# A chunked recurrence in a two-block model: triangular blocks as 32x32 tiles, with their copies shared by two engines

## What is computed

```python
def step(state, inp):
    r_t, w_t, k_t, v_t, kk_t, b_t = inp
    sa = jnp.einsum('bhij,bhj->bhi', state, kk_t)
    state = (state * w_t[:, :, None, :] - sa[..., None] * b_t[:, :, None, :]
             + v_t[..., None] * k_t[:, :, None, :])
    y_t = jnp.einsum('bhij,bhj->bhi', state, r_t)
    return state, y_t
s0 = jnp.zeros((B, H, N, N), f32)
_, y = lax.scan(step, s0, (seq_first(rh), seq_first(wh), seq_first(kh),
                           seq_first(vh), seq_first(kk), seq_first(bh)))
```

## Time and profile before

| | |
|---|---|
| median of 3 runs | 1327.83 us |
| profiled execution, its own time | 1327.68 us |
| its span in the trace | 1325.9 us |
| busy share of PE, DVE, ACT, POOL | 91%, 56%, 46%, 37% |
| mean granted TensorE clock | 0.955 |
| the scan, from its first `w_of` to its last `keep_y` | 330.31 to 454.43 us |

### The profile page before, as it was taken

How to read it: one execution, slowest core, us unless ns; L and a number is a source line. 1 busy time by engine, 2 the same in 40 slices (tenths; PEclk the granted TensorE clock), 3 DMA queues, 4 the chain that set the end, 5 groups by cost and what they waited for, 6 DMA issues and landing times.

```text
span 1325.9 us, 18744 instructions
## 1 busy us (share of the span) xinstructions
PE 1206.0 (91%) x7186; PEld 941.2 (71%) x7186; DVE 745.0 (56%) x1183; ACT 611.1 (46%) x1005; POOL 484.7 (37%) x395
## 2 busy tenths in 40 slices
PE   4699887878999869989999999999999999998977
PEld 4466666656888647777777776777888888876656
DVE  4575996771344373456676657447258234656673
ACT  3576543532222333565655646446111244555664
POOL 1242333426355014433332333434344445532221
PEclk8899898989799879999999999999999999999989
DMA  6642245333010414422222222243233333322101
GB/s 227 216 120 61 58 96 149 111 103 116 10 19 15 145 34 129 134 80 79 64 65 65 64 66 79 80 148 99 72 96 98 99 103 97 95 69 62 48 32 64
DMA packets 198874, 118.13 MB, mean 89 GB/s; under 512 B 27965, under 2 KB 187270, under 8 KB 198534
## 3 DMA queue, kind: packets, MB, share of 16 engines
q1 hardware_dynamic: 194976, 110.58, 28.7%
q10 hardware_dynamic: 3814, 6.40, 1.3%
HBM read 102.28 MB, written 14.68 MB: 88 GB/s over the span
## 4 chain that ended last, share of the span: by engine, by line
PE 37%; issue 24%; POOL 12%; DVE 10%; ACT 2%; POOLq 0%; DMA 0%; ACTq 0%; DVEq 0%
POOL b_w_lo L498 12%; PE banks L587 9%; PE banks L588 9%; PE banks L589 9%; PE banks L856 4%; DVE b_suffix L2403 2%; DVE b_problems L1982 1%; PE banks L831 1%; DVE b_sum_squares L1980 1%; PE banks L1128 1%; PE banks L850 1%; DVE b_softplus L2397 1%; DVE b_sv L2026 1%; PE banks L880 1%; PE banks L940 1%
## 5 line engine op out<-in xcount | busy, mean ns | idle before, releaser
L498 POOL TENSOR_TENSOR b_w_lo<-b_w_raw,b_w_hi 128x512 fp32r<-128x512 f32 x320 | 426.0, 1352 | 762.8 <-ACT b_w_hi L1226 762.8
L587 PE MATMUL banks<-b_a_lo,b_w_hi 128*128 128x512 f32 x1280 | 527.9, 412 | 57.0 <-DVE b_a_lo L1862 20.8
L589 PE MATMUL banks<-b_a_hi,b_w_lo 128*128 128x512 f32 x1280 | 508.0, 397 | 0.0
L588 PE MATMUL banks<-b_a_hi,b_w_hi 128*128 128x512 f32 x1280 | 507.9, 397 | 0.0
L587 PEld LDWEIGHTS banks<-b_a_lo,b_w_hi 128*128 128x128 f32 x1280 | 245.5, 192 | 135.8 <-issue 38.6
L1226 ACT ACTIVATE b_w_hi<-b_w_raw 128x1024 fp32r<-128x1024 f32 x160 | 168.8, 1055 | 267.0 <-PE banks L589 265.9
L589 PEld LDWEIGHTS banks<-b_a_hi,b_w_lo 128*128 128x128 f32 x1280 | 245.6, 192 | 54.4
L588 PEld LDWEIGHTS banks<-b_a_hi,b_w_hi 128*128 128x128 f32 x1280 | 246.6, 193 | 45.5
L1602 ACT ACTIVATE b_exps<-banks,b_stats 128x128 f32<-128x128 f32 (+3 forms) x64 | 33.2, 524 | 58.4 <-DVE b_stats L2197 58.4
L1537 ACT ACTIVATE b_a_hi<-b_x_t,b_params 128x512 fp32r<-128x512 f32 x48 | 33.9, 719 | 53.6 <-DVE b_x_t L2082 53.1
L2082 DVE TENSOR_TENSOR b_x_t<-b_x_t,banks 128x512 f32<-128x512 f32 x32 | 22.0, 686 | 59.7 <-PE banks L589 59.7
(11 more groups left out here) (310 smaller groups left out, 1546.7 us busy)
## 6 DMA issues: line engine op xcount, KB each, us to landing
b_w_raw<-rw_w_in SPq DMA_DIRECT2D x32, 512.0 KB, 4.1
b_w_raw<-da_w_in SPq DMA_DIRECT2D x32, 512.0 KB, 4.0
b_w_raw<-w_in_a SPq DMA_DIRECT2D x32, 512.0 KB, 4.0
b_w_raw<-pe_w_gate SPq DMA_DIRECT2D x16, 512.0 KB, 4.2
d_ple<-b_ple_out ACTq DMA_DIRECT2D x16, 256.0 KB, 2.6
b_w_raw<-rw_w_out SPq DMA_DIRECT2D x8, 512.0 KB, 4.2
b_ple_in<-d_ple SPq DMA_DIRECT2D x2, 2048.0 KB, 10.5
b_w_raw<-da_w_out SPq DMA_DIRECT2D x8, 512.0 KB, 4.0
```

The source lines that it names most:

```text
L498: m = pool.tensor_tensor(WLO[:, u % 2, ks], WRAW[:, u, ks], WHI[:, u % 2, ks].bitcast(F32), ALU.subtract)
L587: pe.matmul(dst, hi, a_lo[:, k_act, :], start=first, stop=False)
L588: pe.matmul(dst, hi, a_hi[:, k_act, :], start=False, stop=False)
L589: return pe.matmul(dst, lo, a_hi[:, k_act, :], start=False, stop=last)
```

## The change

Every block product becomes 16 matmuls with a 32x32 stationary operand, each on its own place in the array, the even head's beside the odd head's. No zeros are loaded, and each of the three steps computes only the half that is used, so `z_of`, `b_of`, `u_of` become `first_u`, `rest_w`, `second_u`. The even heads' W and U now lie in other PSUM banks than the odd heads' (banks 3 and 4, crosswise). Between the steps ACT copies the even heads' 32 rows and DVE the odd heads' 32 rows. The buffer `TRI` holds all chunks' blocks, so it needs no clearing and no reuse: POOL's memsets go, and SP issues all 48 loads in a row; `first_u` of the first chunk waits for 12 of them, that of the third chunk for the other 36. One half of each chunk's output is copied by ACT in place of DVE. DVE's `keep_products` is split into four parts a chunk, which stand between its new copies.

```diff
-    (DBX,) = phase([("blocks", [P, 2, 2, NT, P])], tail_at)
+    (TRI,) = phase([("blocks", [P, NC, 2, NT, BL])], tail_at)
...
         for c in range(NC):
-            if c >= 2:
-                sp.wait_ge(sem("u_mm"), c - 1)
-            got = sem(f"blocks_in{c % 2}")
+            got = sem(f"blocks_in{min(c // 2, 1)}")
             for h in range(2):
...
-                    sp.dma_start(DBX[bp, c % 2, 0, :, bp], D_T[c, :, h, bt, bt].rearrange("j s t -> s j t")).then_inc(got, 16)
...
+                    sp.dma_start(TRI[block_rows(h, b), c, 0], D_T[c, :, h, bt, bt].rearrange("j s t -> s j t")).then_inc(got, 16)
...
-            if 3 <= n < 7:
-                pool.memset(DBX[:, (n - 3) // 2, (n - 3) % 2], 0.0).then_inc(sem("blocks_zero"), 1)
...
-        def block_product(dst, n, c, src, start):
+        def block_product(c, kind, dst, src, start):
+
             for j in range(NT):
-                m = pe.matmul(dst[:, tile_cols(j)], DBX[:, c % 2, n, j, :], src[:, j, :], start=start and j == 0, stop=True,
-                              skip_group_check=True)
+                for h in range(2):
+                    out, bo, rhs, bi = dst(h, j) + src(h, j)
+                    m = pe.matmul(out[block_rows(h, bo), tile_cols(j)], TRI[block_rows(h, bi), c, kind, j, :], rhs,
+                                  start=start and j == 0, stop=True, skip_group_check=True,
+                                  tile_position=(h * CH + bi * BL, h * CH + bo * BL))
             return m
...
+        def first_u(c):
+            if c in (0, 2):
+                pe.wait_ge(sem(f"blocks_in{c // 2}"), 16 * 6 * (2 if c == 0 else NC - 2))
+            pe.wait_ge(sem("w1_kept"), 2 * c + 2)
+            block_product(c, 0, lambda h, j: (UB[h], 0), lambda h, j: (WX[block_rows(h, 0), j, :], 0), True
+                          ).then_inc(sem("u1_mm"), 1)
...
-            z_of(c)
+            first_u(c)
+            if c + 1 < NC:
+                rows_of(c, 0)
+            rest_w(c)
             if c + 1 < NC:
                 products(c + 1, 1)
-            b_of(c)
-            if c + 1 < NC:
-                rows_of(c, 0)
-            u_of(c)
+            second_u(c)
...
             act.wait_ge(sem("w_mm"), c + 1)
-            keep(WX[:, :, :], BANK[3], "w_kept")
-            act.wait_ge(sem("z1_mm"), c + 1)
-            keep(ZX[:, :, :], BANK[4], "z_kept")
-            act.wait_ge(sem("b_mm"), c + 1)
-            keep(WX[:, :, :], BANK[3], "w_kept")
+            keep(WX[first], BANK[3][first], "w1_kept")
+            act.wait_ge(sem("u1_mm"), c + 1)
+            keep(UV[first, :, 0, :], BANK[4][first], "u1_kept")
...
+            act.wait_ge(sem("yx_mm"), c + 1)
+            keep(YT[low, :, c * CH:(c + 1) * CH], BANK[6 + c % 2][low].rearrange("p (j t) -> p j t", t=CH), "y_even")
...
+            dve.wait_ge(sem("w_mm"), c + 1)
+            keep(WX[first], tiles(BANK[4][first]), "w1_kept")
             if c + 1 < NC:
-                for g in range(2):
-                    keep_products(c + 1, g)
-            dve.wait_ge(sem("u_mm"), c + 1)
-            dve.tensor_copy(UV[up, :, 1, :], tiles(BANK[4][up])).then_inc(sem("u_odd"), 1)
+                keep_products(c + 1, 0, 0)
+            dve.wait_ge(sem("u1_mm"), c + 1)
+            keep(UV[first, :, 1, :], tiles(BANK[3][first]), "u1_kept")
             if c + 1 < NC:
+                keep_products(c + 1, 0, 1)
```

More of the change, by code:

```diff
@@ L172, in gn_tile_bank, with block_rows @@
     return (0, 1, 2, 3, 4, 5, 7, 0)[j]
+def block_rows(h, b):
+    return slice(h * CH + b * BL, h * CH + (b + 1) * BL)
 def row(buf, j):
@@ L873, in s_of, with second_u @@
+        def second_u(c):
+            pe.wait_ge(sem("w2_kept"), 2 * c + 2)
+            block_product(c, 0, lambda h, j: (UB[h], 1), lambda h, j: (WX[block_rows(h, 1), j, :], 1), True
+                          ).then_inc(sem("u2_mm"), 1)
         def s_of(c):
@@ L2006, in _, with keep_products @@
         strict = cst("strict_s").unsqueeze(1).to_broadcast([P, 4, CH])
-        def keep_products(c, g):
+        def keep_products(c, g, h):
             dve.wait_ge(sem("x_mm"), 2 * c + g + 1)
-            for h, other in enumerate((up, low)):
-                x = BANK[h].rearrange("p (j n t) -> p j n t", n=2, t=CH)
-                tt(XA[other, 4 * g:4 * g + 4, h, :], x[other, :, 0, :], strict[other], ALU.mult).then_inc(sem("x_kept"), 1)
-                tt(XR[:, c % 2, 4 * g:4 * g + 4, h, :], x[:, :, 1, :], incl, ALU.mult).then_inc(sem("x_kept"), 1)
+            other = (up, low)[h]
+            x = BANK[h].rearrange("p (j n t) -> p j n t", n=2, t=CH)
+            tt(XA[other, 4 * g:4 * g + 4, h, :], x[other, :, 0, :], strict[other], ALU.mult).then_inc(sem("x_kept"), 1)
+            tt(XR[:, c % 2, 4 * g:4 * g + 4, h, :], x[:, :, 1, :], incl, ALU.mult).then_inc(sem("x_kept"), 1)
         def tiles(x):
@@ L2029, in keep_y, with keep @@
             dve.wait_ge(sem("yx_mm"), c + 1)
-            for h, hp in enumerate((low, up)):
-                src = BANK[6 + (h if c % 2 == 0 else 1 - h)]
-                dve.tensor_copy(YT[hp, :, c * CH:(c + 1) * CH], tiles(src[hp])).then_inc(sem("y_done"), 1)
+            src = BANK[7 - c % 2]
+            dve.tensor_copy(YT[up, :, c * CH:(c + 1) * CH], tiles(src[up])).then_inc(sem("y_odd"), 1)
         for g in range(2):
-            keep_products(0, g)
+            for h in range(2):
+                keep_products(0, g, h)
+        first, second = block_rows(1, 0), block_rows(1, 1)
         for c in range(NC):
+            def keep(dst, src, done):
+                dve.tensor_copy(dst, src).then_inc(sem(done), 1)
+            dve.wait_ge(sem("w_mm"), c + 1)
+            keep(WX[first], tiles(BANK[4][first]), "w1_kept")
             if c + 1 < NC:
-                for g in range(2):
-                    keep_products(c + 1, g)
-            dve.wait_ge(sem("u_mm"), c + 1)
-            dve.tensor_copy(UV[up, :, 1, :], tiles(BANK[4][up])).then_inc(sem("u_odd"), 1)
+                keep_products(c + 1, 0, 0)
+            dve.wait_ge(sem("u1_mm"), c + 1)
+            keep(UV[first, :, 1, :], tiles(BANK[3][first]), "u1_kept")
             if c + 1 < NC:
+                keep_products(c + 1, 0, 1)
+            dve.wait_ge(sem("w2_mm"), c + 1)
+            keep(WX[second], tiles(BANK[4][second]), "w2_kept")
+            if c + 1 < NC:
+                keep_products(c + 1, 1, 0)
+            dve.wait_ge(sem("u2_mm"), c + 1)
+            keep(UV[second, :, 1, :], tiles(BANK[3][second]), "u2_kept")
+            if c + 1 < NC:
+                keep_products(c + 1, 1, 1)
                 next_state(c)
```

63 lines of the change are left out of this document (29 added, 34 removed).

## The result

| | before | after |
|---|---|---|
| median of 4 runs | 1328.78 us (1327.46 to 1331.33) | 1310.55 us (1309.76 to 1310.79) |
| profiled execution | 1327.68 us | 1309.76 us |
| span | 1325.9 us | 1308.0 us |
| granted clock, mean | 0.955 | 0.953 |

The ratio is 0.986, with a 95% interval of 0.9842 to 0.9877. Of the 54 executions of the kernel before that ran beside the experiments, one, at 2972.37 us, was in a slow state and is left out of the ratios. The time lies within the range of 1293 to 1317 and 8.5 us above the forecast of 1302.

What follows compares the result with a forecast made beforehand. PE's own work was taken to set the pace of the middle chunks, with short waits. Savings of 14.8 (middle), 5.5 (first) and 5.3 us (last chunk), 25.6 off 1327.68, gave 1302 us; range 1293 to 1317, for 8 in 10.

Steps and rivals of the forecast that it cites:

- The block group: Each group of 16 matmuls with 32x32 operands on PE: 1.15 us until its results, range 0.7 to 2.01.
- The middle chunk: Chunks 1 to 6 of the scan: 11.81 us each in place of 14.27, saving 14.8 us in all.
- The rival with groups of 0.7: Block products on PE: small tiles pack better, 0.7 us a group, 7 us more saved, 1295 us; chance 12%.
- those at the full operands' price: Block products on PE: small tiles cost what full ones do, 21 us come back, 1323 us; chance 5%.
- without overlap: Block products on PE: loads and matmuls run one after another, 4.3 us a group, 1377 us; chance 3%.
- Shape changes: Between PE groups of different shape: 0.17 us idle each, three more a middle chunk, 0.5 us a chunk.
- The copies at the price of their columns: ACT's and DVE's 32-row copies in the solve: time goes with 512 columns, not partitions, so still 0.59 and 0.69 us.
- Memsets and loads at nothing: Ahead of and within the scan: dropping 0.95 us memsets gains nothing, 48 loads cost nothing; late loads had 2%.
- The first chunk: First chunk of the scan, mostly at the 1.2 GHz clock: 17.1 us in place of 22.66, saving 5.5.
- The last chunk: Last chunk of the scan, partly at the lower clock: 10.5 us (9.7 to 11.5) in place of 15.85, saving 5.3.
- Behind the scan: Unchanged work after the scan: taken as 0, with 3 us more as the bound if its first matmuls meet the lower clock.
- The slower rival: Middle chunks lose the full clock: two of six 1315 us, all six 1346; chance 7% for one to three, 4% for more.

Runs made afterwards that it cites:

- the old order: Changed kernel with the fillers put back: second products between first_u and rest_w, first transposes between rest_w and second_u, copies matching; 1311.12 us, ratio 0.9853.
- doubled groups: Changed kernel with first_u and second_u issuing their 16 matmuls twice, rest_w once; 1329.00 us, ratio 0.9981.
- with fillers: Changed kernel with six useless matmuls ahead of the first w_of and two of 256 columns in each of the last chunk's four waits; 1299.47 us, ratio 0.9781.
- the plain pair: Kernel before and changed kernel, both without added POOL memsets ahead of the scan; 1328.78 and 1310.55 us.
- three pairs: Kernel before and changed kernel, each with no, one or three POOL memsets added ahead of the scan; gains 18.2, 25.2 and 23.9 us.
- the loads gated: Changed kernel with block loads issued chunk by chunk, from the third chunk on behind the second_u two chunks back; 1310.44 us, ratio 0.9860.
- the kernel before with fillers: Kernel before with six useless matmuls in PE's waits ahead of the first w_of; 1327.90 us, ratio 0.9982.

## Why the prediction came out as it did, step by step

- **The block group** (1.15 us from L893, 0.7 to 2.01 as bounds): right, 1.04 to 1.08, by the same kind of stream as the row it was read from. The rival with groups of 0.7 and those at the full operands' price or without overlap are out. The prediction took the overlap of loads and matmuls to need the two heads in turn. The full groups of the kernel before, each on all rows of the array, overlap as well: 16 loads of 0.19 us and 16 matmuls of 0.28 us stand within 2.00 us.
- **The middle chunk** (11.81 us): right to 0.04 us. The wait for DVE's copy of U1 was put at 0.2 and is 0.20, that for ACT's copies at 0.28 and is 0.23. The runs with the old order, with all copies on ACT and with doubled groups each moved it the way the steps say: by 0.85 us for 0.63, by 1.2 to 1.3 (at the full clock) for 1.4, and by 1.79 for 2.06.
- **Shape changes** (three more a chunk at 0.17 us, 0.5 in all): over-sized, without effect on the forecast. PE's load queue sits idle for the same 0.17 us behind the products, ahead of a 32x32 group (373.48 in the timeline) as ahead of a full one. Of the three added changes, two stand between a 32x32 group and the transposes and cost about 0.09 each, and one lies within the wait for DVE's copy of U1. The walk had no term for them beside the 1.03 us from group to follower, which measured 1.01, so what the forecast would gain without the rule is not 3 us but some 6 x 2 x 0.09 = 1.1. By the Trainium skill, "TensorEngine Tiling (Array Packing)", Key Properties, a change of tiling mode drains the engine. The trace agrees so far: the next group starts 0.07 us before the last one's end behind a change of shape, and 0.16 before it without one.
- **The copies at the price of their columns**: right, 0.59 and 0.69 for 32 rows.
- **Memsets and loads at nothing**: right for the loads, by their own run. The memsets' going was not run by itself. In the trace of before POOL sat idle for 2.01 us ahead of the operation behind a memset and for 2.90 ahead of those without one, so each memset of 0.95 us stood in a wait.
- **The first chunk** (17.1 us, the clock rising "at the same place"): the term that was mis-sized. It took 18.41, 1.3 more, from two faults. The steps up to `y_state` came to 13.4 us and not 12.7. The block group had been put at 1.75 by the row at 348.54, but the clock rose 1.4 us into that row; wholly at the lower level such a group takes 1.90 (342.85) and the block groups 1.85, three of them, and the transposes 1.04 where 0.85 was taken. And the assumption on the clock was wrong: it rose 2.7 us after `y_state` began and 16.1 into the chunk, and after 3.2 with a delay of 2.6 us, not at an instruction. At the full level the chunk takes 11.78.
- **The last chunk** (10.5 us): mis-sized too, 12.17, outside its own bounds of 9.7 to 11.5. I had taken the low clock for a small part of it; it had 6.6 us of it. At the full level, with fillers, it takes 10.27, against the 9.7 worked out.
- **Behind the scan** (0, with 3 us as the bound): 5.9 us came back, more than the bound, with 10.7 us more of low clock, which at half speed is 5.4 us. That is the larger part of the 7.4 us between the forecast's 25.6 and the 18.2 measured; the first chunk is 1.3 short and the last 1.6, and the stretch ahead of the scan took 0.9 back. The bounds for the clock alone (18.3 for the first chunk, 11.5 for the last, 3 behind) give 1307; that 1310.55 lay in the range owes to the room that it had for slower groups and lost chunks, and to that extent is luck. In the plain pair this falls to the disadvantage of the change; over three pairs the gain is 22.4 us in the mean.
- **The slower rival** (the clock falls in the middle chunks): not in the changed kernel. It came true in the run with all copies on ACT, where PE was busy for 83% of each chunk, after 68 us at the full level.

What stays open: the low clock behind the scan was only recorded, not taken away there. That its length causes the 5.9 us rests on the lengths agreeing (5.4), and on no run in which that part alone was changed. The other traces agree. With the loads gated, the same instructions behind the scan took 873.3 us with 40.4 us of low clock, where the changed kernel took 877.4 with 48.0, and over all fourteen traces the time there goes up by 0.46 us for each microsecond of low clock. Why the first `w_of` stands at 329.4 to 332.1 us where nothing ahead of it was changed, and at 335.0 in the run with all copies on ACT, was not followed.

## What to carry to other kernels

Price an untried tile shape by the row with the same alternation of places, banks and streamed columns, and walk one period through all engines' queues: here that gave the steady chunk to 0.04 us. Keep the steady part of a sum apart from the parts that run while the clock changes, and give those a range of their own: a delay of 2.6 us moved the first chunk by 5.2 and 7.0 us, where the change itself moved it by 4.3. A row that straddles a change of the clock is no price for either level. Where an engine's waits ahead of a dense stretch are known, work of no use in them can be worth more than a further edit: here 6.2 us for six matmuls, against 18.2 for the whole change. It has to be measured in each version, since in the kernel before the same six matmuls gave 0.2%.

## What the runs showed that I had not expected

- A delay did not make the kernel slower: 0.84 us more work on POOL, and 2.6 us less in the median, which the intervals leave open.
- The clock can rise after 3.2 us or after 15.5 to 22.1 us of the same instructions, in both kernels, and neither their place in the span nor their distance from its last fall says which.
- The full level held for 68 us at 83% busy in each chunk and then fell, in the same steady work.
- A scan that got shorter by 6.3 us (the kernel before with fillers, 117.8 against 124.1) left the total shorter by 0.2% only, because the clock fell for longer in the last chunk and behind.
- A 32x32 operand costs 0.028 us a pass in a stream and so hardly less than a 64x64 one at 0.030: of the 0.93 us that a group gained, at most 0.07 (1.15 against 1.08) comes from the tile being smaller than a head, by the row of the 64x64 group; block products with 64x64 operands were not run.
